# A SwiGLU down projection as seven half-size products in place of eight, for 32 of 44 f tiles

## The reference

```
h   = h + merge_groups(...) @ w_out
h   = h + (silu(n @ w_gate) * (n @ w_up)) @ w_down      # n = rms_norm(h, norm2_g)
y   = rms_norm(h, final_norm_g)
```

## Time and profile before

| what | us |
|---|---|
| median of 3 runs (2144.16 to 2145.47) | 2144.52 |
| the profiled execution | 2145.03 |
| its span, first to last instruction | 2143.4 |
| TensorE busy (98% of the span, mean granted clock 0.994) | 2102.3 |
| VectorE busy (61%) | 1305.5 |
| ScalarE busy (35%) | 745.5 |
| GpSimd busy (15%) | 316.2 |
| gate and up, unit 2 to the end | about 765 to 1612.6 |
| down, chunks 0 to 9; then chunk 10 and the final norm | 1612.6 to 2071; to 2143.4 |

### The profile page before, as it was taken

How to read it: one execution, slowest core, us unless ns; L and a number is a source line. 1 busy time by engine, 2 the same in 40 slices (tenths; PEclk the granted TensorE clock), 3 DMA queues, 4 the chain that set the end, 5 groups by cost and what they waited for, 6 DMA issues and landing times.

```text
span 2143.4 us, 42367 instructions
## 1 busy us (share of the span) xinstructions
PE 2102.3 (98%) x17349; PEld 2074.0 (97%) x17349; DVE 1305.5 (61%) x1540; ACT 745.5 (35%) x1056; POOL 316.2 (15%) x292
## 2 busy tenths in 40 slices
PE   7999999999999899999999999999999999999997
PEld 6999999998999899999999999999999999999997
DVE  7653444456543877777777777777775454554455
ACT  4333333234222444444444444444442122222121
POOL 5121212423666300000000000000000000000015
PEclk9999999999999999999999999999999999999998
DMA  8422222332444243333333333333345333432322
GB/s 259 141 80 79 78 78 78 101 99 70 137 132 147 73 134 112 126 118 110 125 119 110 124 121 109 123 122 110 121 164 192 119 116 102 136 118 99 118 79 80
DMA packets 249782, 249.54 MB, mean 116 GB/s; under 512 B 7086, under 2 KB 206358, under 8 KB 249512
## 3 DMA queue, kind: packets, MB, share of 16 engines
q1 hardware_dynamic: 241200, 229.30, 33.3%
q0 software_dynamic: 3360, 12.47, 1.7%
q10 hardware_dynamic: 5160, 6.88, 0.9%
HBM read 223.78 MB, written 26.93 MB: 117 GB/s over the span
## 4 chain that ended last, share of the span: by engine, by line
PE 92%; DVE 5%; DMA 1%; ACT 1%; POOL 1%; issue 1%; ACTq 0%; DVEq 0%; POOLq 0%; SPq 0%
PE pu L894 30%; PE pu L599 22%; PE pu L973 13%; PE pa L973 11%; PE pa L894 8%; PE pa L599 4%; DVE a_hi L1452 1%; PE pa L702 1%; PE pu L722 1%; DVE X L1765 1%; PE pa L711 1%; DVE a_lo L1455 1%; DVE res L1749 0%; DVE a_lo L1550 0%; DVE res L1757 0%
## 5 line engine op out<-in xcount | busy, mean ns | idle before, releaser
L894 PE MATMUL pu<-X,w_hi 128*128 128x260 f32 x3824 | 700.4, 283 | 5.5 <-ACT sg L1347 3.3
L894 PEld LDWEIGHTS pu<-X,w_hi 128*128 128x128 f32 x3824 | 597.1, 189 | 5.9 <-ACT sg L1347 3.5
L894 PE MATMUL pu<-X,w_lo 128*128 128x260 f32 x1912 | 541.9, 283 | 0.0
L1050 ACT ACTIVATE w_hi<-w_raw 128x1024 fp32r<-128x1024 f32 x184 | 184.8, 1052 | 648.0 <-PE pa L973 357.1
L894 PEld LDWEIGHTS pu<-X,w_lo 128*128 128x128 f32 x1912 | 362.1, 189 | 0.1
L1436 DVE TENSOR_TENSOR w_lo<-w_raw,w_hi 128x1024 fp32r<-128x1024 f32 x184 | 239.8, 1345 | 108.3 <-ACT w_hi L1050 108.3
L599 PE MATMUL pu<-a_hi,w_hi 128*128 128x260 f32 (+2 forms) x1312 | 270.8, 288 | 0.8 <-ACT cvs L1095 0.5
L599 PE MATMUL pu<-a_lo,w_hi 128*128 128x260 f32 (+2 forms) x1312 | 265.7, 284 | 0.0
L599 PE MATMUL pu<-a_hi,w_lo 128*128 128x260 f32 (+2 forms) x1312 | 265.2, 284 | 0.0
L599 PEld LDWEIGHTS pu<-a_hi,w_hi 128*128 128x128 f32 x1312 | 203.0, 189 | 13.1 <-issue 11.7
L894 PE MATMUL pa<-X,w_hi 128*128 128x260 f32 x1136 | 214.1, 282 | 0.2 <-DVE w_lo L1709 0.2
(11 more groups left out here) (273 smaller groups left out, 3336.7 us busy)
## 6 DMA issues: line engine op xcount, KB each, us to landing
w_raw<-w_gate SPq DMA_DIRECT2D x44, 1024.0 KB, 5.1
w_raw<-w_down SPq DMA_DIRECT2D x88, 512.0 KB, 4.1
raw_b<-w_up SPq DMA_DIRECT2D x42, 1024.0 KB, 5.1
w_raw<-w_in SPq DMA_DIRECT2D x72, 512.0 KB, 4.9
w_raw<-w_out SPq DMA_DIRECT2D x32, 512.0 KB, 4.1
fraw<-f_t SPq DMA_DIRECT2D x11, 1040.0 KB, 7.5
f_t<-fbuf SPq DMA_DIRECT2D x42, 260.0 KB, 2.1
q_s<-x_t POOLq DMA_DIRECT2D x16, 260.0 KB, 3.5
```

Source lines behind the costliest of these rows:

```text
L894: last = mm(bank, w_slot(w, slot)[:, P * j:P * j + P], X[:, 2 * X_REGION[x] + lo, HT * j:HT * j + HT], start=start and j == 0 and i == 0, ...
L1050: act.activation(w_hi[:, slot, part], w_raw[:, slot, part], ACT.Copy).then_inc(s.hi_made, 1)
```

## The change

Down is done in the order chunk 8, S block 0, chunk 9, S block 1, chunk 10. The S blocks take f tiles 0 to 15 and 16 to 31 as eight units each; a unit is 2048 inputs of w_down (16 f tiles; the halves are the even and the odd tiles) by 256 outputs, in seven products like a fast unit. Chunks 8, 9, 10 (f tiles 32 to 43) stay plain.

- The token operands of an S block are four sums of f (t_t, made by VectorE in gate and up for pairs 0 to 15, kept in tbuf, stored to DRAM) and three plain parts of f_t. Seven loads of 1.07 MB fill them (`load_xd`), ScalarE and VectorE split them during the plain chunk ahead (`xd_hi`, `xd_lo`); the one of product 4 (x4) can be loaded only after that chunk, since f_hi and f_lo lie in its place.
- The weights have one raw set, w_raw: "k0" is A11 and A21 (1 MB), then A12 and A22 (0.5 MB each, rows of 512 bytes). A22 lies in w_raw for even units and in sg0 for odd ones and is loaded a unit further ahead. The residual's place is that of raw_b and the buffers before it.
- u2 and r1 (in the S units) lie in rstd, so unit 2 has no wait for the store of sg0.
- g_fin lies over operands of the last S unit; POOL loads it after that unit's last product.
- The loops of down are gone: all of it is written out.

```diff
+U_S, N_S = 2 * NPAIR, 8
+S_PAIRS = 16
+LAST = (U_S - 1, U_S + N_S - 1, U_S + 2 * N_S - 1)
+D_ORDER = ((2, 3, 0, 1), (0, 1, 2, 3), (0, 1, 2, 3))
+XD_ORDER = (0, 2, 3, 1, 5, 6, 4)
...
-        r1, r5, u2 = rc[:, 0, :], rc[:, 1, :], sg0[:, 0, 0:HT]
+        r1, r5, u2 = rc[:, 0, :], rc[:, 1, :], rstd[:, HT:OUT]
+        r1_d, r1_u2 = rstd[:, 0:HT], rstd[:, 0:OUT]
...
@@ SP @@
+            for sc in range(2):
+                u0 = U_S + N_S * sc
+                load_s(u0 + 1, "a22")
+                sp.wait_ge(s.lo_made, 2 * (U_P3 + 4 * sc + 2) + 2)
+                load_s(u0, "k0")
+                sp.wait_ge(s.lo_made, 2 * (U_P3 + 4 * sc + 3) + 2)
+                load_s(u0, "a22")
+                load_s(u0, "a12")
+                load_xd(sc, 4)
+                for u in range(u0, u0 + N_S - 1):
+                    sp.wait_ge(s.g_lo, form_count(u, 4))
+                    load_s(u + 1, "k0")
+                    sp.wait_ge(s.g_lo, form_count(u, 5))
+                    load_s(u + 1, "a12")
+                    if u + 2 < u0 + N_S:
+                        sp.wait_ge(s.g_lo, form_count(u, 6))
+                        load_s(u + 2, "a22")
...
@@ PE @@
+                form(0)
+                product(chain1, 0, 0, True, x_ready(0))
+                pe.wait_ge(s.c12_made, u - 3)
+                form(1)
+                product(chain2, 1, 1, True, x_ready(1))
+                pe.wait_ge(s.r1_read, u - 1)
+                form(2)
+                product(chain1, 2, 2, False, x_ready(2))
+                form(3)
+                product(single, 3, 3, True, x_ready(3))
+                pe.wait_ge(s.u2_read, u - 1)
+                form(4)
+                product(chain1, 0, 4, False, x_ready(4))
+                pe.wait_ge(s.r5_read, u - 1)
+                form(5)
+                product(chain2, 1, 5, False, x_ready(5))
+                pe.wait_ge(s.c22_made, u - 1)
+                form(6)
+                product(chain1, 2, 6, False, x_ready(6))
+            for sc in range(2):
+                down(sc)
+                for u in range(U_S + N_S * sc, U_S + N_S * sc + N_S):
+                    s_unit(u)
+            c = 2
...
@@ ACT @@
-                if isinstance(u, int) and u == 2:
-                    act.wait_ge(s.f_out, 32)
                 keep(u2, gbank[kind][0], 2, s.u2_read, s.c12_made)
...
@@ DVE @@
+                t_sum(0, part(0, 1), part(0, 0))
+                t_sum(2, part(1, 1), part(0, 1))
+                dve.wait_ge(s.t_made, 4 * g + 1)
+                t_sum(1, part(1, 1), tbuf[:, 0, :])
...
+                t_sum(3, buf[:, 1, 0:HT], tbuf[:, 1, :])
...
@@ DVE @@
+                form_lo_s(u, 4)
+                if first:
+                    xd_lo(sc, 4, 0)
+                    xd_lo(sc, 4, 1)
+                form_lo_s(u, 5)
+                form_lo_s(u, 6)
+                dve.tensor_tensor(top, top, r1_u2, ALU.add).then_inc(s.c11_made, 1)
+                dve.tensor_tensor(r22, r22, r5, ALU.add).then_inc(s.r5_added, 1)
+                if not last:
+                    sum1_s(v)
+                    sum3(v, 0)
+                dve.wait_ge(s.g_done, prod_count(u, 4))
+                dve.tensor_tensor(r22, chain1, r22, ALU.add).then_inc(s.c22_made, 1)
...
+                    form_lo_s(v, 3)
+                    form_lo_s(v, 0)
...
@@ DVE @@
-            c = NCH - 1
+            c = 2
             dve.wait_ge(s.gf_in, 16)
...
@@ POOL @@
-            pool.wait_ge(s.g_lo, form_count(2 * NPAIR - 1, 6))
+            pool.wait_ge(s.g_done, prod_count(LAST[2], 6))
             pool.memset(acc_d[:, :], 0.0).then_inc(s.acc_zeroed, 1)
             pool.dma_start(g_fin[:, :], t["final_norm_g"].rearrange("(o n) -> o n", o=1).to_broadcast([P, D_MODEL])
```

More of the change, by code:

```diff
@@ L519, in _ @@
                 store_f(g, fbuf)
[L521 to L529, removed]
@@ L541, in _ @@
-            load_f(1, 1)
-            store_f(NPAIR - 1, fbuf)
[L544 to L558, removed]
+                store_t(g)
+            with sp.Fori(S_PAIRS, NPAIR - 1) as g:
+                load_pair(2 * g + 2, 0, g + 1, 0, lo_waits(2 * g))
+                load_pair(2 * g + 3, 1, g + 1, 1, lo_waits(2 * g + 1))
+                store_f(g, fbuf)
+            def load_f(ci):
+                sp.wait_ge(s.g_done, prod_count(LAST[ci], 1))
+                sp.dma_start(fraw[:, :, :], t["f_t"][8 + ci].rearrange("f p n -> p f n")).then_inc(s.fr0, 16)
@@ new lines, in _ @@
+            for sc in range(2):
+                start_down(sc)
+                xd_hi(sc, 0)
+                xd_hi(sc, 2)
+                weights(2 * sc + U_P3 // 2 + 1, 0)
+                xd_hi(sc, 3)
+                xd_hi(sc, 1)
+                weights(2 * sc + U_P3 // 2 + 1, 1)
+                xd_hi(sc, 5)
+                xd_hi(sc, 6)
+                for f in range(4):
+                    form_hi_s(U_S + N_S * sc, f)
+                for u in range(U_S + N_S * sc, U_S + N_S * sc + N_S):
+                    s_unit(u)
@@ L1866, in fast_unit @@
                     times_gate(0, 0, s.c11_made, 1)
-                if not nxt:
-                    for k in range(FT):
-                        chunk_lo(0, 0, k)
                 dve.wait_ge(s.g_done, prod_count(u, 4))
@@ new lines, in sum1_s, with down, some @@
+            def sum1_s(u):
+                dve.wait_ge(s.graw00, raw_count(u))
+                dve.wait_ge(a22_in[u % 2], a22_count(u))
+                dve.tensor_tensor(tiles8(S[:, :]), block_of(w_raw, 0, 1), a22_of(u), ALU.add).then_inc(s.s_made, 1)
+            def down(ci):
+                halves_left = [(i, h) for i in XD_ORDER[:6] for h in range(2)]
+                u = U_S + N_S * ci
+                def some(n):
+                    for _ in range(n):
+                        xd_lo(ci, *halves_left.pop(0))
+                for pos in range(4):
+                    if ci == 0 and pos in (0, 2):
+                        dve.wait_ge((s.rd1, s.rd0)[pos // 2], 16)
+                    if pos == 3:
+                        sum2(u, 0)
+                    for o in range(4):
+                        add(ci, pos, o, o)
+                        some(((0, 1, 1, 0), (1, 1, 1, 0), (1, 1, 1, 0), (0, 1, 0, 0))[pos][o])
+                    if pos < 2:
+                        weights(2 * ci + U_P3 // 2 + 1, pos)
+                        some(1)
+                    elif pos == 2:
+                        sum1_s(u)
+                        sum3(u, 0)
+                        some(1)
+                        form_lo_s(u, 0)
+                        form_lo_s(u, 1)
+                form_lo_s(u, 2)
+                form_lo_s(u, 3)
+                dve.wait_ge(s.graw01, raw_count(u))
+                sum4(u, 0)
```

426 lines of the change are left out of this document (308 added, 118 removed).

## The result

The changed kernel took 2097.86 us (median of 4 runs, 2096.93 to 2102.59), the kernel before 2144.99, timed beside it: a ratio of 0.9783, 95% interval 0.9771 to 0.9796. The prediction was 2098.0. The profiled execution took 2096.93 us, its span is 2095.4, so 48.0 less than before's 2143.4.

The account below looks back on a forecast made before the run. TensorE was taken as the bound, with 92% of the chain of waits. From the profiled 2145.03 us, -45.8 (matmuls), -5.1 (unit 2) and +4.4 (g_fin) gave 2098.5, 0.5 less for the median: 2098.0 us, range 2093 to 2110.

Parts of the forecast that it names:

- The matmuls: Down: 384 fewer matmuls at 0.1194 us each, -45.8 us in full if TensorE stays the bound.
- VectorE and ScalarE: S units: VectorE's work takes 14.8 us and ScalarE's 8.6 of a 20.07 us unit, so both fit.
- Unit 2: Gate and up: with u2 in rstd, no wait for the store of sg0; -5.1 us, bounds 3.3 and 5.1.
- The boundaries: Between plain chunks and S units: loads and splits arrive in time, cost 0; upper bound 4.3 us plus a clock loss.
- Rival (b): Chunk and S-unit boundaries: a full queue lands f, x4 or S weights late, 5 to 10 us more; chance 0.18.
- The token sums: End of the up unit: four differences for each of 16 pairs, 1.4 us of VectorE, cost 0.
- g_fin: Last chunk: load lands after 7 us, TensorE stalls 2.7, plus 1.7 clock loss; +4.4 us, bounds 0.6 and 7.6.
- rival (a): Last chunk: g_fin's load lands within 5 us, no stall or clock loss, 2093.6 us; chance 0.12.
- The reload: S units: the single raw weight set is reloaded while the unit computes, in time for the next; cost 0.
- 3 us of cover: S units: form 0's low part done 17.0 us into the unit, wanted at 20.07, absorbing a late sum1.
- (c): S units: VectorE or the reload holds each of 16 units 0.5 to 1.5 us, about 2114 us; chance 0.06.
- (d): S units: exposed reload costs 5.1 us in each of 16, 2180 us; 12.2 us landing decides against; chance 0.04.

Follow-up runs that it names:

- experiment 5: Changed kernel with g_fin's home over operands free earlier, POOL loading it after product 1 of the last unit, not product 6: 2096.56 us.
- experiments 7 and 9: Changed kernel, first-half weight reload issued after form 5's low part instead of form 4's: 2110.85 us; the same with product 4's add moved ahead of sums: 2111.34 us.
- experiments 4 and 11: Changed kernel, VectorE waiting for g_fin before first use, not first add: 2094.60 us; changed kernel, SP loading g_fin ahead of four weight loads: 2094.15 us.
- the repetition: The changed kernel run once more without any edit: 2097.04 us.
- u2_in_sg0: Changed kernel with gate and up's kept sum u2 back in sg0, with the old waits: 2105.62 us.
- experiment 12: Also spelled gf_pool_alone: changed kernel, POOL still loading g_fin, but SP holding its four down weight loads until g_fin has landed: 2096.30 us.
- k0_after_6: Changed kernel with the reload of the raw weights' first half issued after form 6's low part instead of form 4's: 2169.53 us.
- experiment 2: Changed kernel with product 3 of each S unit computed twice, bringing back 16 x 24 matmuls: 2143.71 us.

## Why the prediction was right, step by step

**The matmuls, -45.8**: down up to its last chunk gave -45.9, and putting the count back gave 45.9 to 46.7 back. Right, with TensorE the bound throughout.

**VectorE and ScalarE**: 15.3 and 69.18 / 8 = 8.6 us a unit for 14.8 and 8.6. Right, with VectorE 0.5 under its real load.

**Unit 2, -5.1**: the milestones give -5.10; the upper of its two bounds was the right one, since both the idle time and the clock behind it went.

**The boundaries, 0**: no gap at either. The load of f lands in time with little to spare: experiment 5 put 1 MB beside it and 1.28 us leaked, and in experiments 7 and 9, with later weight loads, chunk 9 began 2.4 and 2.7 us late. Rival (b) was a fair one, and it is nearer than the trace of the changed kernel tells.

**The token sums, 0**: shown by doubling them.

**g_fin, +4.4**: the mechanism held to the row (one gap, two tiles in, released by the add behind the load). Landing 7.3 for 7, idle 3.03 for 2.7. The 1.7 us for the clock did not come in the profiled execution, so the term measured 3.3. By taking the gap away, experiments 4 and 11 give its price on the medians, 2.4 to 3.7 by which median of the changed kernel one takes. In the profiles of the repetition and of u2_in_sg0 the clock did fall behind the same gap and some 1.5 us went, so the 1.7 is a cost that some executions pay, and as a fixed term it was too large. The 7 us had been chosen between bounds by "lighter than the 8.3"; experiments 11 and 12 show what it is made of. With the weight loads held back it is 5.0 us from POOL; issued ahead of them from SP it is 4.3. The Trainium skill's page "DMA: Bandwidth & Descriptors", section "Anatomy of one DMA", has the formula from which the prediction worked out 4.4 us, an estimate. The prediction held this load's 8.3 us against it, but those were for a load with company: alone it took 5.0 in experiment 12, 0.6 over the estimate, so rival (a)'s landing was possible, if not beside four other loads. The same page's section "Queues, rings and completion order" says that a DMA engine takes turns between queue rows, packet by packet; the runs fit this, as a load from POOL shared with SP's, 7.3 us, and one ahead of them in SP's own queue did not, 4.3.

**The reload, 0**: the cost is 0, and the step that argued it is the one that was mis-sized. "3 us of cover" was read off form 0's low part alone, in units of gate and up. In the changed kernel sum 1 waits for its load in three units only; in most it starts at about 12.1 without a wait (12.7 in the first unit of a block), as predicted. One of the three, a unit begun at 1693.16 whose first half took 7.2 us to land, VectorE and then ScalarE:

```profile
1706.17 1.23 DVE L2199 TENSOR_TENSOR S<-w_raw,sg 128x1024 f32<-128x1024 f32 x1 [0.84 <-DMA w_raw<-w_down]
...
1708.45 0.42 DVE L2258 TENSOR_TENSOR res_d<-pa,res_d 128x260 f32<-128x260 f32 x1
1708.80 2.36 DVE L2192 TENSOR_TENSOR w_lo<-w_raw,w_hi 128x1024 fp32r<-128x1024 f32 x2
```

```profile
1707.70 2.01 ACT L1580 ACTIVATE w_hi<-w_raw 128x1024 fp32r<-128x1024 f32 x2 [4.58 <-DMA w_raw<-w_down]
```

Sum 1 starts at 13.0; the add is done at 1708.87, 1.5 us ahead of product 6 (1693.16 + 17.2 = 1710.36); A12 has landed by 14.5, where it must by 16.4; the low parts are done at 18.0 for 20.07. So the cover is 1.5 us by the add and 1.9 by A12 in this unit, and some 2.4 by the add in most. The add on r22 the prediction did not name as a path. A12 it had landing at 13.2, by a landing of 4.9 us; that is this kernel's median too, but its longest is 6.3. The reloads are 14, not the 16 that rivals (c) and (d) count, since the first unit of a block is loaded in the plain chunk.

Rival (d) also had too far a point of decision, 12.2 us from issue to landing. Issuing 2.6 us later (8.4 us into a unit, 1710.29 - 1701.93, in place of 5.8) puts sum 1 at 14.5, right at the limit, and cost 14 us, most of it in the first units. Issuing 5.4 us later (1717.79 - 1706.57 = 11.2) puts it at 17.6, 3 us past the limit in each unit, and cost 72, with the clock loss. A line between those two crosses the 47 us of gain at 4.2 us of delay: a landing of about 10 us in each unit, a rough estimate from these runs (A12 came later in both too), would have undone the change. Rivals (c) and (d) were unlikely for the right reason, the load's usual 5.8 us, and with a wrong margin.

The Trainium skill's page "Trainium Kernel Development and Optimization", section "Best Practices", which tells one to double-buffer, did not decide here: one raw set costs nothing while the load lands in 5.8 us, and 72 us when it, and A12 with it, is issued 5.4 and 3.3 us later.

**The sum.** That 2098.0 and 2097.86 agree to 0.1 us is luck. The profiled execution took 2096.93 where the sum for one is 2098.5: g_fin was 1.1 too dear, and 0.3 were saved ahead of unit 2, which no term has. The median then lies 0.9 above the profiled execution, where the prediction took 0.5 below.

## What to carry to other kernels

When a buffer is reloaded in place, work out the latest start of its first reader along every path behind it, results that merely queue on the same engine included: moving one of two equally late paths out of the way wins nothing. A wait on a late load belongs in front of its first use and its issue ahead of bulk transfers of the same moment; either alone took away a 3 us gap. And price an idle stretch of a saturated TensorE as the stretch plus a clock loss that may or may not come.

## What the hardware showed unexpectedly

The clock behind a gap is not fixed by the gap's length. Behind 3.03 us of idle it stayed at 1.00 in the changed kernel; behind the same gap of 3.00 us in its repetition it was 0.50, and in u2_in_sg0 24 matmuls took 4.40 us for 2.87. In k0_after_6 it was 0.54 behind 2.83 us and 1.00 behind 2.82 us:

```profile
1701.90:1704.90 3.00, 3.00 (x15) 3.00 (x16) 1.51 (x2) 2.61 (x3) 0.00 (x0) 0.54 0.04 11
1704.90:1720.00 15.10, 15.10 (x126) 15.10 (x126) 10.96 (x12) 5.30 (x8) 0.00 (x0) 0.98 0.07 17
...
1966.07:1969.07 3.00, 3.00 (x24) 2.92 (x24) 2.26 (x2) 2.61 (x3) 0.00 (x0) 1.00 0.02 5
```

What decides it was not settled. Nor was the scatter of the changed kernel's times, two of nine of them 3 to 5 us above the rest. It was absent in the five runs each of experiments 4, 5 and 11, which suggests the clock behind g_fin's gap. But gf_pool_alone, with 0.5 us of that gap left, shows it too (2099.45 and 2100.05), and so does the kernel before, which has no such gap: beside experiment 2 four of its 13 runs lie between 2148.30 and 2148.79, at a median of 2144.71.
